# Sparse attention of an 8-head block: scores issued one unit sooner, ScalarE's exponentials ahead of its copies, validity folded into the gates

## The reference

```python
def masked_softmax(s, mask):
    s = jnp.where(mask, s.astype(jnp.float32), -jnp.inf)
    m = jnp.max(s, axis=-1, keepdims=True)
    m = jnp.where(jnp.isfinite(m), m, 0.0)
    p = jnp.exp(s - m)
    return p / jnp.maximum(jnp.sum(p, axis=-1, keepdims=True), jnp.finfo(jnp.float32).tiny)
...
        s_c = jnp.einsum('bqkgd,bnkd->bqkgn', qc, k_cmp) * scale
        mask_c = (cmp_end[None, :] <= t[:, None])[None, :, None, None, :]
        p_c = masked_softmax(s_c, mask_c)
        o_c = jnp.einsum('bqkgn,bnkd->bqkgd', p_c.astype(v_cmp.dtype), v_cmp)
...
        return gc[..., 0:1] * o_c + gc[..., 1:2] * o_s + gc[..., 2:3] * o_w
```

## Time and profile before

| | us |
|---|---|
| median of 3 runs | 2457.86 |
| lowest and highest | 2454.66, 2465.47 |
| profiled execution | 2457.72 |
| its span, first to last instruction | 2455.9 |
| PE busy in the span | 2374.0 (97%) |
| DVE, ACT busy | 1725.2 (70%), 1443.8 (59%) |
| POOL busy | 80.9 (3%) |

### The profile page before, as it was taken

How to read it: one execution, slowest core, us unless ns; L and a number is a source line. 1 busy time by engine, 2 the same in 40 slices (tenths; PEclk the granted TensorE clock), 3 DMA queues, 4 the chain that set the end, 5 groups by cost and what they waited for, 6 DMA issues and landing times.

```text
span 2455.9 us, 32052 instructions
## 1 busy us (share of the span) xinstructions
PE 2374.0 (97%) x12122; PEld 1946.4 (79%) x12122; DVE 1725.2 (70%) x2105; ACT 1443.8 (59%) x1759; POOL 80.9 (3%) x85
## 2 busy tenths in 40 slices
PE   9789999879999999999999999999999999999998
PEld 7468888647888888888888888888878888887886
DVE  7455446637988888888888888857555465755554
ACT  6444444536777777777777777665544445554443
POOL 1100000200100000000000000000000000000000
PEclk9899999889999999999999999999999999999999
DMA  7426555324999999999999999724526542453551
GB/s 258 141 86 206 189 188 157 122 88 160 360 348 371 346 368 349 372 345 369 349 366 352 373 345 370 271 84 161 192 95 205 189 145 97 150 186 110 189 188 43
DMA packets 249560, 569.99 MB, mean 232 GB/s; under 512 B 9648, under 2 KB 20336, under 8 KB 249456
## 3 DMA queue, kind: packets, MB, share of 16 engines
q1 hardware_dynamic: 249456, 568.56, 65.8%
HBM read 562.82 MB, written 1.05 MB: 230 GB/s over the span
## 4 chain that ended last, share of the span: by engine, by line
PE 84%; issue 8%; DVE 4%; ACT 3%; DMA 0%; POOL 0%; SPq 0%; DVEq 0%; POOLq 0%; ACTq 0%
PE PS L912 24%; PE PS L914 23%; PE PS L913 23%; PE PS L1065 2%; PE PS L1077 1%; PE PS L1120 1%; PE PS L1516 1%; ACT SM L1788 1%; PE PS L1346 1%; PE PS L984 1%; PE PS L1103 1%; DVE SM L2359 1%; DVE HTl L2187 1%; DVE SM L2331 1%; PE PS L1009 1%
## 5 line engine op out<-in xcount | busy, mean ns | idle before, releaser
L2574 DVE TENSOR_TENSOR Wl<-ring,Wh 128x2048 fp32r<-128x2048 f32 x334 | 762.0, 2299 | 101.0 <-ACT Wh L1925 101.0
L1925 ACT ACTIVATE Wh<-ring 128x2048 fp32r<-128x2048 f32 x334 | 639.9, 1919 | 127.8 <-PE PS L914 127.8
L2180 DVE TENSOR_TENSOR Wl<-ring,Wh 128x2048 fp32r<-128x2048 f32 (+2 forms) x192 | 431.2, 2251 | 281.5 <-ACT Wh L1695 281.0
L1695 ACT ACTIVATE Wh<-ring 128x2048 fp32r<-128x2048 f32 (+2 forms) x192 | 361.6, 1890 | 234.9 <-PE PS L914 233.8
L912 PE MATMUL PS<-Wh,HTh 128*128 128x512 f32 (+3 forms) x1184 | 464.4, 392 | 4.7 <-DVE Wl L2180 2.4
L914 PE MATMUL PS<-Wh,HTl 128*128 128x512 f32 (+3 forms) x1184 | 456.4, 385 | 0.0
L913 PE MATMUL PS<-Wl,HTh 128*128 128x512 f32 (+3 forms) x1184 | 455.4, 385 | 0.0
L912 PE MATMUL PS<-Wh,xgh 128*128 128x512 f32 x896 | 354.4, 396 | 1.8 <-DVE Wl L2574 1.2
L914 PE MATMUL PS<-Wh,xgl 128*128 128x512 f32 x896 | 349.5, 390 | 0.0
L913 PE MATMUL PS<-Wl,xgh 128*128 128x512 f32 x896 | 348.9, 389 | 0.0
L912 PEld LDWEIGHTS PS<-Wh,HTh 128*128 128x128 f32 x1184 | 222.8, 188 | 51.0 <-issue 5.0
(11 more groups left out here) (336 smaller groups left out, 2455.6 us busy)
## 6 DMA issues: line engine op xcount, KB each, us to landing
ring<-in_moe_w_gate SPq DMA_DIRECT2D x112, 1024.0 KB, 6.8
ring<-in_moe_w_up SPq DMA_DIRECT2D x112, 1024.0 KB, 7.1
ring<-in_moe_w_down SPq DMA_DIRECT2D x112, 1024.0 KB, 6.8
ring<-in_mlp_w SPq DMA_DIRECT2D x64, 1024.0 KB, 5.2
ring<-in_w_in SPq DMA_DIRECT2D x27, 1024.0 KB, 5.3
ring<-in_w_out SPq DMA_DIRECT2D x16, 1024.0 KB, 7.2
ring<-in_cross_wkv SPq DMA_DIRECT2D x16, 1024.0 KB, 12.3
ring<-in_ffn_w_gate SPq DMA_DIRECT2D x14, 1024.0 KB, 5.1
```

The lines of the kernel that those rows point to most:

```text
L1695: act.activation(Wh[:, i % SPLITS, 0:n], ring[:, r % RING, 0:n], ACT.Copy).then_inc(w_hi, 1)
L1925: act.activation(Wh[:, (base + i) % SPLITS, :], ring[:, (raw + i) % RING, :], ACT.Copy).then_inc(e_hi, 1)
L2180: dve.tensor_tensor(Wl[:, i % SPLITS, 0:n], ring[:, r % RING, 0:n], Wh[:, i % SPLITS, 0:n].bitcast(F32), ALU.subtract).then_inc(w_lo, 1)
L2574: dve.tensor_tensor(Wl[:, (base + i) % SPLITS, :], ring[:, (raw + i) % RING, :], Wh[:, (base + i) % SPLITS, :].bitcast(F32), ALU.subtract) ...
```

## The change

Five edits, in the sparse attention alone; the other attentions of the kernel keep their order.

1. PE's round i issues scores(i+1) in place of scores(i), ahead of the transposes of unit i-1.
2. ACT's round is exps(i), then copies(i-1).
3. The compressed keys: their product comes ahead of the last half product, ACT takes them ahead of exps(0), DVE squares them in `between(0)` and norms them in `between(1)` (before: 1 and 2), their transpose rides with unit 1 (before: 2).
4. glu(1) stands between mask(1) and weigh(0) (before: behind weigh(0)). POOL's multiplications still wait for the last half product, which is now the layer's twelfth `lin_full` (before: the eleventh).
5. `cvalid` multiplies the gates of the compressed branch once for each tile, ahead of glu(0); L2357 goes.

The diff, cut to its core:

```diff
-        nsa_extras = {0: t_conv, 2: [t_kc]}
+        nsa_extras = {0: t_conv, 1: [t_kc]}
...
-                pool.wait_ge(lin_full, layer * LIN1 + 11)
+                pool.wait_ge(lin_full, layer * LIN1 + 12)
...
+                    ahead_ = 1 if units[0]["end"][0] == "nsa" else 0
                     for i in range(1, n + 2):
-                        if 2 <= i < n:
-                            scores(i)
+                        if 2 <= i + ahead_ < n:
+                            scores(i + ahead_)
...
                 begin()
-                half_products(1, 1, w).then_inc(lin_full, 1)
...
                 mm.then_inc(lin_full, 1)
-                finish({2: rows})
+                half_products(1, 1, w).then_inc(lin_full, 1)
+                finish({1: rows})
...
+                if units[0]["end"][0] == "nsa":
+                    for i in range(n + 1):
+                        if i < n:
+                            exps(i)
+                        if i >= 1:
+                            copies(i - 1)
+                        if i in meanwhile:
+                            meanwhile[i]()
+                    return
...
-                attention(nsa_units(), nsa_extras, {7: lambda: mix_of(0)},
-                          {1: lambda: take(kc_sb[0:NCMP, :, :].rearrange("p a b -> p (a b)"), rows=NCMP)})
+                take(kc_sb[0:NCMP, :, :].rearrange("p a b -> p (a b)"), rows=NCMP)
+                c.lin += 1
+                attention(nsa_units(), nsa_extras, {7: lambda: mix_of(0)})
...
-                    if br == 0:
-                        seq(dve.tensor_scalar(cf, cf, cvalid[:, un["t"]:un["t"] + 1], None, ALU.mult))
...
                     if i < count:
                         mask(i)
+                    if i in early:
+                        early[i]()
...
+                for t in range(T):
+                    shares = proj[:, t, GATE0:GATE0 + 3 * HEADS].rearrange("p (h b) -> p h b", b=3)[:, :, 0]
+                    dve.tensor_scalar(shares, shares, cvalid[:, t:t + 1], None, ALU.mult)
...
-                    if i == 1:
-                        glu(1)
-                        c.lin += 1
-                        dve.wait_ge(lin_out, base + 12)
+                    if i == 0:
+                        dve.wait_ge(lin_out, base + 11)
...
-                    elif i == 2:
+                    elif i == 1:
                         power()
...
-                attention(nsa_units(), nsa_extras, between)
+                def second_glu():
+
+                    c.lin += 1
+                    glu(1)
+
+                attention(nsa_units(), nsa_extras, between, {1: second_glu})
```

More of the change, by code:

```diff
@@ L575, in plan @@
                 c.raw += 2
-                c.lin += 1
+                c.lin += 1 + 1
                 linear([IN1_BLOCKS[4][1]])
-                c.lin += 1 + 3
+                c.lin += 3
                 linear([512])
@@ L1492, in _ @@
                 cmp_lin = c.lin
-                banks = [lin_bank() for _ in range(T)]
+                banks = [lin_bank()]
+                kc_bank = lin_bank()
                 def half_products(half, t, w):
@@ L1552, in _ @@
                 compress(cmp_bank)
+                banks.append(lin_bank())
                 half_products(0, 1, w).then_inc(w_half, 1)
@@ L1556, in _ @@
                 w = split_slot(piece(), HALF, n)
-                kc_bank = lin_bank()
                 added(cmp_lin)
@@ L2031, in _ @@
                 turn(t_nsa)
-                c.lin += 2
+                c.lin += 1
                 act.wait_ge(turned, c.turn + 1)
@@ L2311, in rotate_copies, with attention @@
                     last.then_inc(signal, 1)
-            def attention(units, extras={}, between=None):
+            def attention(units, extras={}, between=None, early={}):
                 u0, count = c.unit, len(units)
```

## The result

| | before | after |
|---|---|---|
| median, us | 2457.37 | 2430.17 |
| lowest and highest of 4 executions | 2454.66, 2465.47 | 2428.00, 2431.86 |
| profiled execution | 2457.72 | 2431.16 |
| its span | 2455.9 | 2429.2 |
| mean granted clock | 0.988 | 0.989 |

The ratio is 0.9883, with a 95% interval of 0.9859 to 0.9908. The forecast was 2421, with a range of 2407 to 2436: the time lies inside it, 9 us above the forecast's own value. The gain is 27.2 us where 37.0 were forecast.

A forecast was written before the change was run, and what follows sets the result against it. No single engine was taken as the bound: TensorE, VectorE and ScalarE wait in a ring in both layers' sparse attention. Layer terms of -17.7 and -19.3 make -37.0 from 2457.7, given as 2421 us, range 2407 to 2436.

The forecast's parts named there:

- The ring: Sparse attention loop: scores one unit sooner cut TensorE's waits from 16.0 to 3.0 us, left before units 7 and 10.
- The scores that leave the loop: Layer 0's loop: scores(3) now stand ahead of unit 1's transposes, taking 1.09 us off TensorE's busy time.
- ScalarE's order: Loop: exponentials ahead of copies delay copies by at most 2.0 us, their readers come a round later; cost none.
- Validity: Gates: eight VectorE operations of 0.23 us go, four small ones come, none on the path; 0, between -0.5 and +0.6.
- The opening: Before unit 1's transposes: VectorE slowed beside GpSimd's multiplications, transposes at 82.2 in place of 81.6; +0.6 us.
- All blocked: Opening's upper bound: VectorE blocked by GpSimd until 78.5, unit 1's transposes at 83.4, +1.8 us.
- nothing blocked: Opening's lower bound: GpSimd blocks no VectorE operation, unit 1's transposes at 76.9, -4.7 us.
- SP's queue: Opening: 16 shift DMAs go out about 2 us later, 7 if GpSimd blocks everything; no cost, worst case 1 us.
- The clock: TensorE's low level: 4.1 us a layer goes with removed waits, 2.4 after the opening stays, 1.6 goes behind layer 1.
- The first rival: GpSimd blocks everything (+2.4), the clock falls as often as before (+8.2), the spill stays (+1.6): 2433 us; 14%.
- The forecast's own sign of being wrong: Among the signs listed against the forecast: granted clock below 0.9 beyond 90 us.
- the fifth rival: Slower: the clock does not come back after the opening's waits, loop at 1.2 GHz, +16 us a layer, 2489 us; 3%.

The follow-up runs named there:

- e_scores_late: Changed kernel with TensorE issuing scores(i) again in place of scores(i+1), ScalarE's new order kept; 2465.6 us, one run.
- e_fill_both: Changed kernel plus unread TensorE products in the opening's two waits and in the wait before unit 10's transposes; 2414.3 us.
- e_cvalid_back: Changed kernel with validity multiplied into the compressed branch's coefficient in each of its units again, not into the gates; 2428.7 us.
- e_pool_late: Changed kernel with GpSimd's four convolution-weight products held back until VectorE has weighted unit 1's tile; 2412.2 us.
- e_all: Changed kernel with GpSimd's convolution weights held back until unit 1 is weighted, plus unread TensorE products in the opening and before unit 10; 2407.2 us.

## Why the prediction was right, and where it was 9 us off

- **The ring** was right in its mechanism, place and size. Forecast: no wait but 1.2 us before unit 7 and 1.5 before unit 10, 3.0 in all. Measured: 1.23, 1.52, 2.75 in all. Going back in one line (e_scores_late) brings 15.1 us of waits again.
- **The scores that leave the loop** (1.09 us) were right: they no longer stand in the loop. The work at full clock in e_fill_both's loop is 43.9 us, though, 1.2 below the 47.5 - 2.4 = 45.1 of the forecast. The forecast had counted 6.5 us of low level in the loop before (4.1 + 2.4), and it was 7.6; scores(3) themselves took 1.57 us there and not 1.09. (47.5 and 3.0 of waits make 50.5, not 50.4.)
- **ScalarE's order** at no cost was right in its sign. That the ring's 3.0 us need it, and that it is worth some 8 us beside the early scores (one run), the text didn't say.
- **Validity** at nothing, between -0.5 and +0.6: e_cvalid_back shows no difference in time, and 0.27 us a layer in the wait before unit 10. "None on the path" was wrong for that one unit, the bounds were right.
- **The opening** was right: +0.6 forecast, +1.0 measured in layer 0. Unit 1's transposes stand at 82.64, where 82.2 was forecast from one operation of VectorE passing at each end of a GpSimd multiplication. The four operations ended at 73.0, 75.4, 77.3 and 79.3, forecast 72.9, 74.8, 76.7 and 78.5; the rest took 3.4 us, as its terms have it (0.7 + 1.05 + 1.63). These terms add to 81.9, not 82.2, so the true miss is 0.8, and it lies in GpSimd's 8.01 us instead of 7.51. "All blocked" (83.4; its terms make 83.6) and "nothing blocked" (76.9) were both wrong as forecasts; the second is what e_pool_late reaches (76.69).
- The Trainium skill's rule ("SBUF — State Buffer", section "Who interferes with whom") that a VectorE operation with two SBUF inputs and a GpSimd one that reads SBUF exclude each other fits the coefficient product, 1.10 against 0.17 us, and the tile, 2.36 against 0.69. It did not make the upper bound come true, since between GpSimd's four multiplications VectorE got in.
- **SP's queue** at no cost: right. The first shift DMA went out at 78.17 instead of 74.33, 3.8 us later where about 2 were forecast, and no half of the convolution waited for one.
- **The clock** is the step that failed. The forecast took off 4.1 us a layer for low stretches "after waits that go", kept 2.4 for the one after the opening, and took off 1.6 behind layer 1, -9.8 in all. Measured: +0.8, from the two loops and w_out. Of the 4.1 only the 3.2 behind units 3 and 7 went (96 to 128 us stands at 1.00). The other 0.9, values(9), and the 1.6 in w_out could not be counted on by the forecast's own waits: that low stretch stands behind the wait before unit 10, which the ring's count keeps at 1.5 us. It measured 1.68 before and 1.52 after, and the stretch behind it grew and reached 6 us into w_out in both layers. In layer 0 the stretch after the opening grew too: unit 1's transposes to the end of the first convolution half held 9.7 us of work against 5.35 at full clock in e_fill_both, 4.3 over, where 2.4 had been kept. Without these 9.8 us the same sum gives 2430.5, and 2430.2 was measured; so near a hit is partly luck, since the measured parts differ from the forecast's by up to 1 us each and cancel. The first rival had this mechanism (+9.8), by another way (GpSimd blocking everything); only its half on the clock came true. The forecast's own sign of being wrong, a granted clock below 0.9 beyond 90 us, is there from 128 to 144.
- In the text of the fifth rival stands that a closer-packed loop gains by the rule that activity raises the clock and idling lowers it (the Trainium skill, "TensorE: Matmul & The Clock Gate", "What's actually happening"). Every fall here does lie behind idle time, but the rule didn't give the size: with 2.75 us of waits in layer 0's loop the low level cost 7.8 us, with 16.0 it had cost 7.6.

## What to carry to other kernels

When several engines wait for each other in a ring, and one has work that is free to move, put the step that closes the ring ahead of that work, and count each round as VectorE's part against TensorE's; here that gave the waits to 0.3 us. But don't credit a change with a low stretch unless it removes the wait ahead of that stretch: here each wait that stayed could pull the level down for 8 to 14 us behind it. Where a wait of 1 to 3 us has to stay, products that nobody reads, no longer than the wait, delayed nothing and gave back 16 us here, though not every filled wait kept the level; too long, or in a round without a wait, they give most of the gain back (2457.6 against 2441.3, where no filling had 2465.6).

## What the hardware showed that was not expected

- The low level costs far more than the wait before it: 1.52 us of waiting stand ahead of unit 10, and filling them with 1.56 us of unread work took 10.8 us off the kernel (two layers, 5.4 each).
- Executions of one kernel spread with it: e_pool_late took 2409.7 to 2419.7 us at mean clocks of 0.997 to 0.992, and e_all, whose waits in the attention of layer 0 are 1.3 us at most but for one of 1.71 before unit 2, 2407.0 to 2407.9.
- VectorE's small operations lose most beside GpSimd in proportion: 0.17 us became 1.10, and a 15x128 product 1.99 instead of 0.27. Moving 8 us of GpSimd's work by 6 us took 7.1 us off the kernel at full clock.
